# A separate step order for each engine in the sample stage, which also takes over the end of the last prompt tile

## The reference, cut to what matters

```python
def step(S, inp):                                   # RWKV-7, per token
    sa = einsum('bhij,bhj->bhi', S, -kk_t)
    S = S * w_t + sa (kk_t * a_t) + v_t k_t
    return S, einsum('bhij,bhj->bhi', S, r_t)
yn = (y - mu) * rsqrt(var + GN_EPS) * gn_g + gn_b   # over each head
o_rw = (yn + bonus) * g
s = (q_nope . k_nope + q_rope . k_rope) * ATTN_SCALE    # MLA, keys = 256 past + 16 new for a sample
o_at = rmsnorm(softmax(s) @ v) * mla_out_g
mix = concat([o_rw, o_at]) @ w_out
```

## Time and profile before

| | us |
|---|---|
| median of 3 runs | 2146.5 (2144.93 to 2150.54) |
| the profiled execution | 2147.14, its span 2145.1 |
| from PE's last prompt product to its first sample product | 17.4 |
| sample stage, first to last DMA issue before the next stage | 1039.36 to 1189.19 |
| busy over the span: PE, DVE, ACT, POOL | 1930.8, 938.6, 670.3, 357.2 |

### The profile page before, as it was taken

How to read it: one execution, slowest core, us unless ns; L and a number is a source line. 1 busy time by engine, 2 the same in 40 slices (tenths; PEclk the granted TensorE clock), 3 DMA queues, 4 the chain that set the end, 5 groups by cost and what they waited for, 6 DMA issues and landing times. The chain is left out here.

```text
span 2145.1 us, 39570 instructions
## 1 busy us (share of the span) xinstructions
PE 1930.8 (90%) x16671; PEld 1647.6 (77%) x16671; DVE 938.6 (44%) x1835; ACT 670.3 (31%) x1316; POOL 357.2 (17%) x333
## 2 busy tenths in 40 slices
PE   6999976898889899888497799999999999999995
PEld 6999973676667666666375588999999999999994
DVE  7610114446666665564312365433354333543335
ACT  2221211234434444433121202333343333433331
POOL 0000014322232222121100032311003110031010
PEclk9999996688999999998765899999999999999998
DMA  6352111100211011010400622444444444444441
GB/s 217 132 197 89 45 43 46 43 28 20 74 57 50 9 56 56 2 56 11 134 2 20 239 105 69 130 124 128 126 118 148 136 127 127 118 147 137 124 131 40
DMA packets 167890, 196.28 MB, mean 92 GB/s; under 512 B 18786, under 2 KB 142458, under 8 KB 166580
## 3 DMA queue, kind: packets, MB, share of 16 engines
q1 hardware_dynamic: 165124, 184.77, 27.4%
q0 software_dynamic: 2624, 9.50, 1.1%
HBM read 165.82 MB, written 29.25 MB: 91 GB/s over the span
## 5 line engine op out<-in xcount | busy, mean ns | idle before, releaser
L664 DVE TENSOR_TENSOR c_wo_lo<-c_raw,c_wo_hi 128x1024 fp32r<-128x1024 f32 x96 | 117.6, 1225 | 465.9 <-ACT c_wo_hi L591 465.7
L803 PE MATMUL c_pY<-c_wo_hi,c_hl 128*128 128x512 f32 x576 | 226.1, 392 | 0.0
L803 PE MATMUL c_pY<-c_wo_lo,c_hh 128*128 128x512 f32 x576 | 225.8, 392 | 0.0
L803 PE MATMUL c_pY<-c_wo_hi,c_hh 128*128 128x512 f32 x576 | 225.3, 391 | 0.0
L591 ACT ACTIVATE c_wo_hi<-c_raw 128x1024 fp32r<-128x1024 f32 x96 | 101.8, 1061 | 332.1 <-PE c_pY L803 332.1
L547 POOL TENSOR_TENSOR c_hid<-c_relu 128x384 f32<-128x384 f32 x96 | 79.4, 827 | 677.3 <-ACT c_relu L606 677.3
L835 PE MATMUL c_pU<-c_zT_hi,c_wo_hi 128*128 128x384 f32 x768 | 151.2, 338 | 1.6 <-DVE c_zT_lo L659 1.6
L835 PE MATMUL c_pU<-c_zT_lo,c_wo_hi 128*128 128x384 f32 x768 | 148.6, 334 | 0.0
L835 PE MATMUL c_pU<-c_zT_hi,c_wo_lo 128*128 128x384 f32 x768 | 148.5, 334 | 0.0
L835 PEld LDWEIGHTS c_pU<-c_zT_hi,c_wo_hi 128*128 128x128 f32 x768 | 137.9, 188 | 9.7 <-DVE c_zT_lo L659 2.7
L835 PEld LDWEIGHTS c_pU<-c_zT_hi,c_wo_lo 128*128 128x128 f32 x768 | 134.5, 188 | 0.0
(11 more groups left out here) (452 smaller groups left out, 3431.1 us busy)
## 6 DMA issues: line engine op xcount, KB each, us to landing
c_raw<-w_down SPq DMA_DIRECT2D x96, 512.0 KB, 3.6
c_raw<-w_up SPq DMA_DIRECT2D x96, 512.0 KB, 4.7
scratch_p<-a_o SPq DMA_DIRECT2D x72, 154.0 KB, 1.8
a_w<-w_in SPq DMA_DIRECT2D x8, 1232.0 KB, 7.9
m_prev<-scratch_p SPq DMA_DIRECT2D x8, 896.0 KB, 5.0
m_pr<-scratch_p SPq DMA_DIRECT2D x5, 1232.0 KB, 5.5
b_pr<-scratch_p SPq DMA_DIRECT2D x4, 1232.0 KB, 5.3
scratch_h<-a_x POOLq DMA_DIRECT2D x9, 512.0 KB, 3.8
```

What stands on the lines that cost most here:

```text
L664: dve.tensor_tensor(row_lo[U % 2], row_raw[U % 2][:, :], row_hi[U % 2].bitcast(F32), ALU.subtract).then_inc(S("row_lo"), 1)
L803: last = pe.matmul(pY[2 * t + half][:, :], x, w[:, 512 * half:512 * half + 512], start=first and a == 0, stop=final and a == 2, skip_group ...
```

## The change

1. `sample_steps(engine)` returns a list for PE, one for DVE and one for ACT. POOL has its few steps written out.
2. The order of the work differs. On PE `gram` is split into `gram_x` and `gram_q` (the latter behind `absorb`), `own` into `own_z` and `own_y`, `turn` into `turn_a` (before `queries`) and `turn_b`. In the attention the unit of `request(v)` is score v+2, weights v+1, context v. On DVE, `mean` stands behind `update 0`, `variance` and `gate_out` behind the last `weights`.
3. `pick` takes KT and RT in one product: they lie in one tile `KR`, so that one loaded state block serves 32 columns (2x16) where it served 16 twice.
4. The last prompt tile's `mean`, `variance`, `gate_out` and `finish` leave the prompt stage. The sample stage does them at its start on the tiles kept in `M` (`squares_8`, `mean_8`, `variance_8`, `gate_out_8`; one reciprocal root over 9 columns instead of two). The tile is stored by SP later in the stage, behind the loads of `lat`. The prompt stage ends without them.
5. `state` (four) and `ropeT` are issued by ACT, at the head of its program. SP issues `lat` only when the product of the second squaring (`("X", 1)`) has been evicted.
6. ACT evicts the nope part of the turned queries, which DVE did. The ring has 6 banks; `values` takes its bank from the ring.

```diff
@@ schedule @@
-    return steps + [(s, count - 1, None) for piece in norm for s in piece]
+    return steps
@@ phase_mix_prompt, sync @@
-            store_mix(NP - 1)
             sp.wait_ge(S("state_ready"), chunk_no(NP - 1, 1) + 2)
...
-            sp.wait_ge(S("mix_stored"), 16 * (NP - 1))
+            sp.wait_ge(S("mix_stored"), 16 * (NP - 2))
@@ sample_steps @@
-    steps = plain("turn_latent", "queries", "turn", "gram") + [("newton_t", 0)] + plain("own") + [("newton_x", 0)]
-    steps += plain("turn_queries") + [("newton_t", 1)] + plain("absorb") + [("newton_x", 1)]
-    steps += [("score", 0), ("newton_t", 2), ("score", 1), ("newton_x", 2)] + plain("pick") + attend(0)
-    steps += plain("pick_turn") + attend(1) + plain("scan_sa") + attend(2) + plain("scan_y") + attend(3)
-    steps += [("update", 0)] + plain("mean") + attend(4) + [("update", 1)] + plain("variance") + attend(5)
-    return steps + plain("gate_out") + attend(6) + attend(7) + plain("values")
+    def request(v, beside=()):
+
+        return [("score", v + 2), ("weights", v + 1), ("context", v)] + plain(*beside)
+
+    if engine == "tensor":
+        steps = plain("turn_latent", "turn_a", "queries", "turn_b", "gram_x", "turn_queries", "absorb", "gram_q")
+        steps += [("newton_t", 0)] + plain("own_z") + [("newton_x", 0)] + plain("own_y") + [("newton_t", 1), ("score", 0)]
+        steps += [("newton_x", 1), ("score", 1), ("newton_t", 2)] + plain("pick") + [("newton_x", 2), ("weights", 0)]
+        steps += request(0, ["pick_turn"]) + request(1, ["scan_sa"]) + request(2, ["scan_y"])
+        steps += request(3) + [("update", 0)] + request(4) + [("update", 1)] + request(5)
+        return steps + [("weights", 7), ("context", 6), ("context", 7), ("values", None)]
+    if engine == "vector":
+        steps = plain("mean_8", "init", "turn_a", "variance_8", "gate_out_8", "turn_b", "gram_x", "turn_queries", "gram_q")
+        steps += [("newton_t", 0), ("newton_t", 1), ("score", 0), ("weights", 0), ("score", 1), ("newton_t", 2), ("weights", 1)]
+        steps += [("score", 2), ("weights", 2), ("score", 3), ("weights", 3)] + plain("scan_sa")
+        steps += [("score", 4)] + plain("scan_y") + [("weights", 4), ("score", 5), ("weights", 5), ("update", 0)]
+        steps += plain("mean") + [("score", 6), ("weights", 6), ("update", 1), ("score", 7), ("weights", 7)]
+        return steps + plain("variance", "gate_out", "values")
+
+    steps = plain("turn_latent", "squares_8", "turn_a", "queries", "turn_b", "turn_queries", "absorb")
+    steps += [("newton_x", 0), ("newton_x", 1), ("score", 0), ("score", 1)] + plain("pick") + [("newton_x", 2), ("weights", 0)]
+    steps += [("score", 2), ("weights", 1), ("context", 0)] + plain("pick_turn")
+    for v in range(1, DEC_B - 2):
+        steps += [("weights", v + 1)] + plain("mean") * (v == 4) + [("score", v + 2), ("context", v)]
+    return steps + [("weights", 7), ("context", 6), ("context", 7), ("values", None)]
@@ phase_mix_sample @@
-        J = Jobs(S, [psum(f"s_R{i}", [P, 512]) for i in range(5)], "s")
+        J = Jobs(S, [psum(f"s_R{i}", [P, 512]) for i in range(6)], "s")
...
-                    banks = [J.fill(pe, name) for name in ("zT", "yT")]
-                    for x, src in enumerate((KT, RT)):
+                    for m in range(2):
+                        bank = by_side(J.fill(pe, ("zy", m)))
                         for b in range(B):
-                            for k in range(PAIRS):
+                            for k in range(2):
                                 for g in range(2):
-                                    r, at = slice(HD * g, HD * g + HD), P * k + T * b
-                                    last = pe.matmul(banks[x][r, at:at + T], state[r, k, b, :],
-                                                     src[r, k, T * b:T * b + T], start=True, stop=True)
+                                    r, at = slice(HD * g, HD * g + HD), slice(T * b, T * b + T)
+                                    last = pe.matmul(bank[r, k, :, at], state[r, 2 * m + k, b, :], KR[r, :, 2 * m + k, at],
+                                                     start=True, stop=True)
@@ sync @@
-            sp.dma_start(ropeT[:, :, 0:PAST], io["cache_ropeT"].rearrange("b r n -> r b n")).then_inc(S("ropeT_landed"), 16)
-            for g in range(PAIRS):
-                sp.dma_start(state[:, g, :, :], io["state"][:, P * g:P * g + P, :].rearrange("b p v -> p b v"))\
-                  .then_inc(S("state_landed"), 16)
             for b in range(B):
                 sp.dma_start(lat_new[:, b, :], c[T * b:T * b + T, :]).then_inc(S("latnew_landed"), 16)
+            J.wait_taken(sp, ("X", 1))
             sp.dma_start(lat[:, 0, :, :],
...
+            sp.wait_ge(S("rw_last"), 1)
+            sp.wait_ge(S("at_last"), 1)
+            sp.dma_start(io["mix"][SEQ - P:SEQ, :], mixed[:, :]).then_inc(S("last_stored"), 16)
@@ scalar @@
+            for g in range(PAIRS):
+                act.dma_start(state[:, g, :, :], io["state"][:, P * g:P * g + P, :].rearrange("b p v -> p b v"))\
+                   .then_inc(S("state_landed"), 16)
+            act.dma_start(ropeT[:, :, 0:PAST], io["cache_ropeT"].rearrange("b r n -> r b n")).then_inc(S("ropeT_landed"), 16)
+                if s == "squares_8":
+
+                    junk = ctxT[:, 0].rearrange("p h b t -> p (h b t)")[:, 0:W]
+                    act.activation(junk, mixed[:, W:2 * W], ACT.Square, accum_out=ssq[:, 1:2]).then_inc(S("osq_last"), 1)
+                    act.wait_ge(S("yc_last"), 1)
+                    act.activation(last_y[:, :], last_z[:, :], ACT.Square).then_inc(S("ysq_last"), 1)
+                    act.wait_ge(S("osq_last"), 1)
```

More of the change, by code:

```diff
@@ L2028, in turns @@
                 J.filled(last)
-            for step, v in sample_steps():
+            for step, v in sample_steps("tensor"):
                 if step == "turn_latent":
@@ L2080, in _ @@
-                if step == "own":
-                    for out, w, name in ((Z, CM, "XC"), (Y, QM, "QP")):
-                        for g in range(2):
-                            J.wait_taken(pe, (name, g))
-                        for h in range(HEADS):
-                            for j in range(N_SIDE):
-                                pe.matmul(out[quarter(j), HD * h:HD * h + HD], w[quarter(j), h, :],
-                                          pr[quarter(j), 2 * W + HD * h:2 * W + HD * h + HD],
-                                          start=h == 0, stop=False, skip_group_check=True)
+                    name = "XC" if step == "gram_x" else "QP"
@@ new lines, in _ @@
+                    for g in range(2):
+                        J.filled(ends[g])
+                if step in ("own_z", "own_y"):
+                    out, w, name = (Z, CM, "XC") if step == "own_z" else (Y, QM, "QP")
+                    for g in range(2):
+                        J.wait_taken(pe, (name, g))
+                    for h in range(HEADS):
+                        for j in range(N_SIDE):
+                            pe.matmul(out[quarter(j), HD * h:HD * h + HD], w[quarter(j), h, :],
+                                      pr[quarter(j), 2 * W + HD * h:2 * W + HD * h + HD],
+                                      start=h == 0, stop=False, skip_group_check=True)
@@ L2277, in _ @@
                                                bank[:, 0:4 * QH].rearrange("p (h d) -> p h d", d=QH), ACT.Copy), ("q", g))
-                if s == "turn":
+                if s == "turn_a":
                     bank = J.take(act, "KT")
-                    J.taken(act.activation(KT[:, :, :], four(bank), ACT.Copy), "KT")
+                    J.taken(act.activation(KT, four(bank), ACT.Copy), "KT")
+                if s == "turn_b":
                     bank = J.take(act, "BT")
@@ L2283, in _ @@
                     J.taken(act.activation(BTn, four(bank), ACT.Copy, scale=-1.0), "BT")
+                if s == "turn_queries":
+                    for g in range(2):
+                        bank = J.take(act, ("qT", g))
+                        act.activation(qnopeT[:, 4 * g:4 * g + 4, :], four(bank, NOPE), ACT.Copy).then_inc(S("qnope_out"), 1)
                 if s == "absorb":
@@ L2291, in _ @@
                 if s == "pick":
-                    for x, name in enumerate(("zT", "yT")):
-                        bank = J.take(act, name)
-                        J.taken(act.activation(zyT[x][:, :, :], four(bank), ACT.Copy), name)
+                    for m in range(2):
+                        bank = J.take(act, ("zy", m))
+                        J.taken(act.activation(zyT[:, 2 * m:2 * m + 2], by_side(bank), ACT.Copy), ("zy", m))
                 if s == "pick_turn":
```

146 lines of the change are left out of this document (87 added, 59 removed).

## The result

| | before | after |
|---|---|---|
| median of 4 runs, us | 2145.72 | 2098.78 |
| lowest to highest | 2142.06 to 2150.54 | 2094.21 to 2103.14 |
| profiled execution, us (its span) | 2147.1 (2145.1) | 2094.21 (2092.4) |

The ratio is 0.9776 with a 95% interval of 0.9754 to 0.9798: 46.9 us saved, where 33.5 were forecast. The predicted 2113.0 is 14.2 us too high; the range of 2088 to 2130 holds the time.

What follows compares the result with a forecast made beforehand. PE and its waits were taken to bound the sample stage; seam -15.3, ACT's issues +8.7, gram to weights -11.8 and attention -15.1 sum to -33.5 us, giving 2113.0 us after 0.6 off for the median, range 2088 to 2130.

Steps and rivals of the forecast that it cites:

- The seam: Prompt stage to sample stage: moving the last tile's closing chain out starts the sample stage earlier, -15.3 us.
- the case of -11.9: Seam: smaller saving if the barrier cost the whole 4.7 us between DVE's end and the next stage's first DMA.
- ACT's issues: Sample stage's start: five DMAs at the head of ACT's program hold it about 10 us, costing +8.7 us.
- a free ACT's gain: Start of gram: with ACT free at 2.95 us, gaps of 2.04 and 2.4 return, leaving only 2.6 us lower.
- Gram to the weights: Gram to first attention weights: gaps -9.6, lat gap +2.0, halved pick -4.9, absorb's wait +0.7; sum -11.8 us.
- The gap term: Gram to first weights: PE's three issue gaps vanish, -9.6 us; a new gap at lat's request costs 2.0.
- PE short of instructions, whose own transfers stand in the same DMA engines: Reading of PE's idle gaps while large loads run; gaps staying without any load would prove it wrong.
- The attention: First weights to values: the new order removes PE's three waits for DVE's division, -15.1 us.
- a clock mixed as today: Main forecast's assumption that the attention keeps PE's mixed clock, 0.62; chance 0.42.
- all at the high level: Clock rival: the attention runs wholly at the high clock, 16.7 us less, 2096.3 us; high clock's chance 0.17.
- Lockstep: Slower rival: each of eight attention streams waits for its own score-to-division chain, 68 us, so 2181; chance 0.03.
- re-formed waits: Rival: the 15.1 us of division waits stand elsewhere and the lat gap comes whole, 2131.3 us; chance 0.02.

Runs made afterwards that it cites:

- chain_in_prompt: Changed kernel with the last prompt tile's closing chain put back into the prompt stage; median 2111.3 us, ratio to before 0.9838.
- variance_early: Changed kernel with DVE's update 1 and variance moved ahead of weights 6 again; median 2111.5 us, ratio to before 0.9814.
- old_attention: Changed kernel with the attention in the old common order on PE, ACT and DVE; median 2128.5 us, ratio to before 0.9887.
- sp_rotate_first: Changed kernel with ropeT and state issued by SP, and POOL rotating q before its multiply; median 2089.4 us, ratio to before 0.9706.
- loads_on_sp: Changed kernel with ropeT and state issued by SP again; median 2090.1 us, ratio to before 0.9744; repeated at 2091.6 us, 0.9731.

## Why the prediction was right, and where a term was mis-sized

**The seam** (-15.3): -15.2 measured, and `chain_in_prompt` gives it back. The stage starts 1.41 us after DVE's end, where 1.33 was taken; the case of -11.9 is out.

**ACT's issues** (+8.7): ACT was held 9.96 us, where 10 was chosen between 2.95 and 15.6; that choice was an estimate, and with `state` and `ropeT` taking each other's shares its closeness is in part luck. The stretch grew by 7.4, as the way from the first eviction to gram took 9.57 us, not the 10.9 of before. That the cost is ACT's is shown by three kernels without it. The Trainium skill, in "DMA: Bandwidth & Descriptors", section "Issuing engines are not separate DMA queues", says that the issuing sequencer's time is usually small beside the DMA itself. This trace agrees for `state` (3.56 us of ACT for four DMAs, each with 10.1 us from issue to landing) and not for `ropeT` (6.33 us of ACT, 16.4 to landing); and small or not, 9.9 us of ACT stood on PE's path. That gaps would eat a free ACT's gain in part was right in kind: 5.3 to 8.1 of 11.3 us went again, though the prediction's sentence on it expected 2.6 us net and the five stretches together show 3.5 and 6.5.

**Gram to the weights** (-11.8): -13.2. `pick` went from 11.9 to 7.0 us (-4.9 forecast and measured). The gap term was wrong in its parts: the three gaps did not go whole, and the gap for `lat` did not come. PE's idle time in the stretch fell from 10.34 to 5.24 us, -5.1, where -9.6 + 2.0 + 0.7 = -6.9 was the sum; but busy time outside `pick` fell by 3.2, which no term foresaw. It lies in `absorb`: the same 32 products took 7.19 us in before, at a clock of 0.50 right behind the gap of 5.16, and 3.81 in the changed kernel, at 1.00 (its row stands under the loads). The row of before:

```profile
1072.21 7.19 PE L2061 MATMUL s_R<-s_qT,s_both 64*128 64x128 f32 x32
```

The reading "PE short of instructions, whose own transfers stand in the same DMA engines" fell in part by the prediction's own test: gaps of 2.1 and 1.1 us stay with a DMA share of 0.00. That loads can lengthen them stands; that they are PE's supply of instructions was not shown by any run.

**The attention** (-15.1): -29.5, and this is the mis-sized term. The waits themselves were sized rightly: idle time fell from 16.06 to 1.10 us, -15.0. The step that failed is "a clock mixed as today", which priced a change of clock at nothing. PE's busy time fell by another 14.6 us for the same products, at a clock of 0.87 instead of 0.62. The prediction had this as a rival, "all at the high level", at 16.7 us and a chance of 0.17: 2096.3, and the eight executions of the changed kernel have a median of 2095.9. That they agree so well is luck: the clock did not reach the high level throughout, and small terms elsewhere made up for it. The range holds the time because its lower end had been set by this rival. The rival was held down by the earlier trace rows, a stretch at 0.50 with 16.96 of 19 us busy. That stretch followed the wait of 8.5 us, and `variance_early` shows what that means: it is the part in which the clock has fallen and not yet risen. The rows should have been read by what stood ahead of them, not as a sample of the attention without waits. The clock is not explained by waits in the attention alone. In the changed kernel it lay at 0.50 from 1062 to 1089, with PE busy nearly all the time and no gap longer than 2.05 us ahead of it since gram:

```profile
1062.00:1089.00 27.00, 26.93 (x369) 20.80 (x369) 3.70 (x13) 5.52 (x16) 0.00 (x0) 0.50 0.33 104
```

The same attention, without a long wait, had clocks from 0.87 to 1.00 in ten profiled executions, and took 38.7 to 44.1 us by it. What decides between these is open.

The Trainium skill says in "TensorE: Matmul & The Clock Gate", section "What's actually happening", that activity releases the throttle. That was nearer than the forecast: PE was busy 6.00 of 6.00 us in the slices in which the clock rose from 0.50 to 0.89 and 1.00. The row above shows that it does not say when. `old_attention` shows the waits' part from the other side: with them back the clock is 0.59.

**The rest.** The tail's zero was -1.1. Lockstep and re-formed waits did not come: the longest wait for a division is 0.5 us.

## What to carry to other kernels

A wait of several microseconds on TensorE's path can have two prices, its own length and the slower clock of the work behind it. Here they were 15.0 and 14.6 us for three waits, and 5.8 and 6.9 us for one. So a change that removes the last long wait of a stretch is to be costed with and without the second price. The second is the less certain: one kernel had longer gaps ahead of its attention and yet the highest clock in it. A stretch that is busy and still slow is to be read together with the pause that stood before it. DMA issues moved to a compute engine are work of that engine: count them in its program, and put them where they delay nothing that is needed soon.

## What the runs showed of the hardware that was not expected

The same five DMAs held SP for 13.0 us, ACT for 9.9 and POOL for 4.3. On SP `ropeT` took 3.60 and `state` 9.40 us, on ACT 6.33 and 3.56; but in `chain_in_prompt`, also on ACT, it was 3.90 and 5.60, so the split is not one of the engine.

Executions of one kernel differ by up to 18 us (before, in one series, by 23), and in the one high execution that was profiled most of it is not in the sample stage. `sp_rotate_first` was profiled at 2102.1 us, while its other three took 2083.8 to 2090.2. Its last prompt product ends at 1031.44, in `loads_on_sp` (2088.9) at 1020.14, with the same program in the prompt stage. One window of each, `sp_rotate_first` first:

```profile
500.00:600.00 100.00, 88.45 (x1209) 64.74 (x1207) 56.99 (x141) 41.81 (x114) 22.97 (x22) 0.85 0.12 41
```

```profile
500.00:600.00 100.00, 87.74 (x1298) 64.41 (x1296) 62.18 (x158) 43.46 (x117) 26.77 (x25) 0.93 0.12 41
```

At a clock of 0.85 in place of 0.93 some 90 fewer products were started in these 100 us. Its attention, 39.7 us at 0.97, was shorter than that of `loads_on_sp`. The cause of that clock is not known from these runs, and whether the other high executions have the same one was not seen.
